# Experts ordered on chip by rising token count, with 64 more rows in the last eight places

## The chip, the cores and the metric

One core of one Trainium2 chip. The metric is device time in microseconds (us) of one execution of the whole kernel, lower is better. Engines by their names in the profile: PE is TensorE (PEld its weight loads), DVE is VectorE, ACT is ScalarE, POOL is GpSimd, SP is SyncE; a name with a small q is that engine's queue.

## What is computed

One layer of an encoder trunk, float32, 1024 tokens of width 1024. A mixer (neighbourhood attention, a bidirectional RWKV-7 scan, cross attention into memory tokens) comes first and is not touched by the change. Behind it stands a mixture of experts:

```python
g_idx = argmax(h2 @ w_group + b_group)                 # 1 of 4 groups
top_p, top_i = top_k(softmax(logits of that group), 2) # 2 of its 4 experts
weights = g_w[:, None] * top_p / sum(top_p)
expert = g_idx[:, None] * 4 + top_i                    # 2 of 16 experts per token
hid = silu(xb @ w_gate[e]) * (xb @ w_up[e])            # 1024 -> 512
y[token] += (hid @ w_down[e]) * weight                 # 512 -> 1024
```

2048 (token, expert) pairs fall on 16 experts, 128 each on average; how many each one gets is known only on chip. An expert's three matrices are 2 MB each.

## The kernel before

The mixer takes the first 690 us or so. Then `out_projection_router` computes the output projection, the rows for the experts and the routing, in four pairs of 128-token tiles. For each pair `place` (line 1690 on) gives every (token, expert) pair a slot, 1024 slots per expert, and GpSimd scatters one entry of eight words per pair into `tok_dram` (line 1576): token row, half-row numbers, weight. `s.count` is kept on VectorE and holds, in the end, each expert's number of rows.

`experts` (line 1824 on) has two parts.

**The fixed part** runs over 16 experts in the order `EXPERTS`: expert i of group 0, of group 1, 2, 3, then i + 1. Each multiplies exactly its first 128 slots; slots that nobody filled hold entries whose writes are dropped. On TensorE expert e is: gate (L2038), transposes of the hidden block of expert e - 1 (`turn_h`, L2016), up (L2046), transposes of the next expert's rows (`turn_x`, L2008), down of expert e - 1 (L2026). Gate and up matrices have three buffers (`GU_SETS`), down matrices two. SyncE loads gate and up of expert e once gate and up of expert e - 3 are done; ScalarE loads down of e once down of e - 2 is done, and does SiLU and the copy of the transposed hidden block. VectorE does the product `hid`, the copy of the transposed rows, and `finish`: weight times product plus the output rows read back. GpSimd's queue holds, per expert: `read_rows` (output rows, L1918), `expert_rows` (gather of input rows, L1821, waits for `turn_x` two experts on), in experts 6 to 13 four `entries` each (a register read and two small DMAs with the slots of a possible overflow block, L1932 to L1934), and `write_rows` (L1924).

**The overflow part** takes what exceeds 128, in blocks of 64 rows. `overflow_blocks` and `overflow_rows` compute on VectorE, early in the fixed part, how many blocks there are and which expert and slots each has (`s.blk`). Every engine then runs a loop of 6 turns with 6 places, each place in an `If` (`overflow`, line 1882 on). A block loads its expert's three matrices again. Its products are 64 rows tall: two halves of the columns go to the two 64-row halves of the result (L2073, L2080, L2097; a block is 32, 32 and 16 matmul instructions in the profile). Blocks are chained by the output: the half rows are read from the output (L1987), summed (L2236), written (L1995), and the next block's read waits for that write.

```python
for q in range(COLS):
    mm = pe.matmul(pg[q * ROW:(q + 1) * ROW, 0:256], xoT[:, j, :], wg[g][:, j, q * 256:(q + 1) * 256],
                   start=(j == 0), stop=(j == KD - 1))
```

Of the kernel before, what the change touches and what calls it, by code (L numbers as in the profile page):

```python
# [62 lines left out]
EXPERTS = [NE // NG * g + i for i in range(NE // NG) for g in range(NG)]  # L63
# [1433 lines left out]
def out_projection_router(nc, s):  # L1497
# [4 lines left out]
    with ExitStack() as c:  # L1502
# [20 lines left out]
        slotf = sb("slotf", [P, 2, 2])  # L1523
        unused = sb("unused", [P, 16, ENTRY], I32)
# [18 lines left out]
        def _(sp):  # L1543
# [8 lines left out]
            for load in expert_loads(s, EXPERTS[0], 0, 0):  # L1552
                load(sp)
            expert_loads(s, EXPERTS[1], 1, 1)[2](sp)
            for t in range(TT):
                if t == TT - 1:
                    sp.wait_ge(done, 2 * TT)
                    for load in expert_loads(s, EXPERTS[1], 1, 1)[0:2]:
# [74 lines left out]
        def _(dve):  # L1633
# [69 lines left out]

            link(dve.memset(unused[:, :, :], 0))
# [62 lines left out]
            place(PAIRS - 1)  # L1767

# [56 lines left out]
def experts(nc, s):  # L1825
# [4 lines left out]
    with ExitStack() as c:  # L1830
# [6 lines left out]
        acc, acc_o = s.proj[:, 2:4, :], s.proj[:, C_ALL - 1, 0:512]  # L1837
        weight = s.idx[:, :, WEIGHT].bitcast(F32)
        idx_u = sb("idx_u", [P, TURN, ENTRY], I32)
# [24 lines left out]
        idx_in = sem("idx_in")  # L1864
        xo_in = [sem(f"xo_in{u}") for u in range(2)]
# [26 lines left out]
        def _(sp):  # L1892
            tok = s.tok_dram.rearrange("(g i r) c -> i r g c", g=NG, i=NE // NG)
# [4 lines left out]
            for e in range(2, NE):  # L1898
                for load, used in zip(expert_loads(s, EXPERTS[e], e % GU_SETS, e % 2)[0:2], (gated, upped)):
                    if e >= GU_SETS:  # L1900
                        sp.wait_ge(used, e - GU_SETS + 1)
                    load(sp)

            def load_weights(b, i, third, turn):
                e = sp.value_load(s.blk[0:1, ds(b, 1)], min_val=0, max_val=NE - 1)
                for load, used in zip(expert_loads(s, e, (NE + turn) % GU_SETS, turn % 2)[0:2], (gated, upped)):
                    sp.wait_ge(used, b + (NE - GU_SETS + 1))
# [4 lines left out]
        def _(pool):  # L1912
# [31 lines left out]

            pool.wait_ge(s.idx_first, 16)
# [5 lines left out]
            pool.wait_ge(s.idx_rest, 16 * NE // NG)  # L1951
# [4 lines left out]
            for e in range(NE):  # L1956
# [10 lines left out]
                if e == NE - 2:  # L1967
                    pool.wait_ge(zeroed, 2)
                    pool.wait_ge(idx_in, 32 * NOV)
                    for b in range(2):  # L1970
                        take(b, b, b + 1)
                        gather(b)
                    pool.sem_inc(xo_turned, 1)
                if e in RECLAIM:
                    pool.drain()
                if e == NE - 1:
                    pool.wait_ge(xo_turned, 2)
                    take(2, 2, 3)
                    gather(2)
                    n = overflow_count(pool)  # L1980
                write_rows(e)
            for g in range(NG):
                pool.wait_ge(s.row_written[g], 16 * NE // NG)

            def rest(b, i, third, turn):
                u = turn % 2
                pool.indirect_dma_start(out=acc_o, out_offset=None, in_=halves,  # L1987
                                        in_offset=bass.IndirectOffsetOnAxis(ap=idx_u[:, turn, HALF_READ:HALF_READ + 1], axis=0)).then_inc(s.half_in[u], 16)
                pool.wait_ge(xo_turned, b + 3)
# [3 lines left out]
                pool.wait_ge(summed_o, b + 3)  # L1993
# [3 lines left out]
                pool.wait_ge(s.row_written_o[u], i * 16 + 16)  # L1997
# [4 lines left out]
        def _(pe):  # L2002
            def turn_x(e):
                pe.wait_ge(x_in[e % 2], e // 2 * 16 + 16)
                if e:
                    pe.wait_ge(x_copied, e)
                for j in range(KD):
                    mm = pe.transpose(pt[:, j // 4, (j % 4) * P:(j % 4 + 1) * P], x[:, e % 2, j * P:(j + 1) * P], s.ident)  # L2008
                mm.then_inc(x_turned, 1)

            def turn_h(e):
                pe.wait_ge(hidden, e + 1)
                if e:
                    pe.wait_ge(h_copied, e)
                for j in range(KF):
                    mm = pe.transpose(ph[:, j * P:(j + 1) * P], hid[:, j * P:(j + 1) * P], s.ident)  # L2016
                mm.then_inc(h_turned, 1)

            def down(e):
                pe.wait_ge(h_copied, e + 1)  # L2020
                pe.wait_ge(wd_in[e % 2], e // 2 * 16 + 16)
                if e:
                    pe.wait_ge(summed, e)
                for half in range(2):
# [4 lines left out]

            turn_x(0)  # L2030
            for e in range(NE):
                u, g = e % 2, e % GU_SETS
                pe.wait_ge(x_copied, e + 1)
                pe.wait_ge(wg_in[g], e // GU_SETS * 16 + 16)
                if e:
                    pe.wait_ge(silu, e)
                for j in range(KD):
                    mm = pe.matmul(pg[:, :], xT[:, u, j, :], wg[g][:, j, :], start=(j == 0), stop=(j == KD - 1))  # L2038
                mm.then_inc(gated, 1)
                if e:  # L2040
                    turn_h(e - 1)
                pe.wait_ge(wu_in[g], e // GU_SETS * 16 + 16)
                if e:
                    pe.wait_ge(hidden, e)
                for j in range(KD):
# [4 lines left out]
                if e:  # L2050
                    down(e - 1)

            def turn_rows(u, part):
                for j in range(4 * part, 4 * part + 4):
                    mm = pe.transpose(pt[:, j // 4, (j % 4) * P:(j % 4 + 1) * P], xo[:, u, j * P:(j + 1) * P], s.ident)
                return mm

            turn_h(NE - 1)
            pe.wait_ge(xo_in[0], 16)
            turn_rows(0, 0)  # L2060
            turn_rows(0, 1).then_inc(xo_turned, 1)
            n = overflow_count(pe)
            down(NE - 1)

            def block_of_rows(b, i, third, turn):
                u, g = turn % 2, (NE + turn) % GU_SETS
                fixed = len(range(g, NE, GU_SETS))
                pe.wait_ge(xo_copied, b + 2)
                pe.wait_ge(wg_in[g], third * 16 + 16 * (fixed + 1))
                pe.wait_ge(silu_o, b + 1)  # L2070
                for j in range(KD):
                    for q in range(COLS):
                        mm = pe.matmul(pg[q * ROW:(q + 1) * ROW, 0:256], xoT[:, j, :], wg[g][:, j, q * 256:(q + 1) * 256],  # L2073
# [326 lines left out]
```

## Time and profile before

| what | value |
|---|---|
| runs shown (3) | 1269.63, 1271.72, 3097.08 us |
| median of the runs | 1271.72 us |
| span of the profiled execution, first to last instruction | 1268.2 us |
| TensorE busy | 1175.8 us, 93% |
| VectorE, ScalarE, GpSimd busy | 551.6, 308.4, 203.2 us |
| moved by the DMA engines | 242.40 MB |
| fixed part of the experts, first gate to last down product | about 821 to 1177 us |
| overflow blocks | 5 |

The profile gives no other time for the profiled execution than its span; launch and end around it are in the runs' times only. Busy times of TensorE are modelled at their ends, so consecutive groups overlap by some 0.2 us; start-to-start times are the better ones. A DMA's duration is from its issue to its landing.

### The profile page before, as it was taken

What the parts mean: (1) busy time and instruction counts of PE and PEld (TensorE: products, weight loads), DVE (VectorE), ACT (ScalarE), POOL (GpSimd) and SP (SyncE); (2) the same over time, 40 slices, a digit from 0 to 9 for tenths busy, and PEclk for the clock granted to TensorE, in tenths of its full rate; (3) what the DMA queues carried; (4) which work ended last, traced back from release to release, by engine and by line L of the source; (5) the groups of instructions that cost most, each with busy time, mean ns of one, the idle gap of its engine ahead of it and who ended that gap; (6) DMA issues with size and microseconds to landing.
All of it is one profiled execution on the core that took longest, in us unless ns stands there. A gap on an engine that the chain in (4) does not pass through costs nothing. (4 is left out here: it accounts for less than half of the span.)

```text
span 1268.2 us, 24058 instructions
## 1 busy us (share of the span) xinstructions
PE 1175.8 (93%) x9814; PEld 660.0 (52%) x9814; DVE 551.6 (43%) x1316; ACT 308.4 (24%) x791; POOL 203.2 (16%) x250
## 2 busy tenths in 40 slices
PE   6999999999998888999999999399999999999785
PEld 5534444444444666899974555244444444444442
DVE  4358356899793555555745344302211111111111
ACT  5153116322212666433431222000000000000000
POOL 0201310300001334000000011401102242332122
PEclk9999999999998999999999999599999999999988
DMA  9311521222203723144344612688989999999973
GB/s 319 99 38 48 180 68 55 103 97 100 51 34 90 187 78 110 50 114 113 104 168 170 265 67 77 238 322 326 368 353 353 365 340 372 347 369 326 390 263 128
DMA packets 110055, 242.40 MB, mean 191 GB/s; under 512 B 36404, under 2 KB 71684, under 8 KB 104568
## 3 DMA queue, kind: packets, MB, share of 16 engines
q1 hardware_dynamic: 82696, 150.30, 33.3%
q0 software_dynamic: 16688, 48.59, 10.9%
q10 hardware_dynamic: 10560, 41.94, 9.9%
q8 instruction: 79, 1.29, 0.4%
q14 instruction: 32, 0.26, 0.1%
HBM read 211.25 MB, written 36.10 MB: 195 GB/s over the span
## 5 line engine op out<-in xcount | busy, mean ns | idle before, releaser
L505 PE MATMUL pj_ps<-hT,pj_w 128*128 128x512 f32 x576 | 253.0, 595 | 0.0
L505 PEld LDWEIGHTS pj_ps<-hT,pj_w 128*128 128x128 f32 x576 | 107.8, 190 | 135.4 <-issue 134.9
L1387 PE MATMUL ps_out<-w_out,mixT 128*128 128x512 f32 x256 | 112.3, 594 | 2.1 <-PEq L2315 1.8
L2026 PE MATMUL ex_py<-wd,ex_hT 128*128 128x512 f32 x256 | 112.6, 593 | 0.2 <-DVE proj L2169 0.2
L2206 DVE TENSOR_TENSOR ex_hid<-ex_pu,ex_sg 128x512 f32<-128x512 f32 x16 | 11.1, 692 | 205.5 <-PE ex_pu L2046 205.5
L2122 ACT ACTIVATE ex_sg<-ex_pg 128x512 f32<-128x512 f32 x16 | 9.6, 597 | 324.4 <-PE ex_pg L2038 324.4
L2038 PE MATMUL ex_pg<-proj 128*128 128x512 f32 x176 | 80.2, 610 | 1.3 <-DVE proj L2162 1.3
L1387 PEld LDWEIGHTS ps_out<-w_out,mixT 128*128 128x128 f32 x256 | 47.8, 190 | 59.5 <-issue 59.4
L715 DVE RECIPROCAL mixT<-mixT 128x1024 f32<-128x1024 f32 (+1 forms) x11 | 68.9, 6262 | 22.5 <-ACT mixT L635 17.5
L2046 PE MATMUL ex_pu<-proj 128*128 128x512 f32 x176 | 77.3, 592 | 0.0
L2026 PEld LDWEIGHTS ex_py<-wd,ex_hT 128*128 128x128 f32 x256 | 47.5, 190 | 54.4 <-issue 54.0
L1576 POOL DMA_INDIRECT slot_tokens<-op_entry,op_slot x16 | 15.6, 975 | 287.9 <-DVE op_slot L1701 284.2
L2169 DVE SCALAR_TENSOR_TENSOR proj<-ex_py,idx,proj 128x1024 f32<-128x1024 f32 x16 | 20.5, 1284 | 91.7 <-PE ex_py L2026 91.7
L2038 PEld LDWEIGHTS ex_pg<-proj 128*128 128x128 f32 x176 | 34.4, 196 | 45.1 <-issue 43.4
L509 PE MATMUL pj_ps<-proj,hT 128*128 128x512 f32 x128 | 55.5, 594 | 0.0
L1924 POOL DMA_INDIRECT out<-proj,idx x16 | 16.4, 1026 | 241.8 <-DVE proj L2169 241.8
L2046 PEld LDWEIGHTS ex_pu<-proj 128*128 128x128 f32 x176 | 32.7, 190 | 37.3 <-issue 37.3
L1277 DVE TENSOR_TENSOR wd<-sc_ps,cst 128x384 f32<-128x384 f32 x64 | 35.7, 557 | 32.1 <-PE sc_ps L1214 31.1
L1210 PE MATMUL sc_ps<-proj 64*64 64x128 f32 x512 | 40.8, 270 | 1.0 <-PEq L1181 1.0
L509 PEld LDWEIGHTS pj_ps<-proj,hT 128*128 128x128 f32 x128 | 24.2, 190 | 30.5 <-issue 30.5
L1077 DVE CUSTOM_DVE_ANT_0 at_ssb<-at_ps_s,at_table 128x253 f32<-128x253 f32 (+1 forms) x64 | 24.0, 408 | 33.3 <-issue 33.3
L1117 ACT ACTIVATE at_pr<-at_ssb,at_nm 128x253 f32<-128x253 f32 (+1 forms) x64 | 31.4, 492 | 21.7 <-DVE at_nm L1077 14.6
(324 smaller groups left out, 1959.2 us busy)
## 6 DMA issues: line engine op xcount, KB each, us to landing
wd<-in_moe_w_down ACTq DMA_DIRECT2D x20, 2048.0 KB
proj<-in_moe_w_gate SPq DMA_DIRECT2D x14, 2048.0 KB, 10.5
proj<-in_moe_w_up SPq DMA_DIRECT2D x14, 2048.0 KB, 9.3
mixT<-in_moe_w_gate SPq DMA_DIRECT2D x7, 2048.0 KB, 10.8
mixT<-in_moe_w_up SPq DMA_DIRECT2D x7, 2048.0 KB
pj_w<-in_w_in SPq DMA_DIRECT2D x18, 512.0 KB, 3.8
proj<-in_x SPq DMA_DIRECT2D x16, 512.0 KB, 10.2
products<-pj_unit POOLq DMA_DIRECT2D x4, 2048.0 KB, 10.1
```

What stands on the lines that cost most here:

```text
L505: mm = pe.matmul(ps[:, t % 2, half, :], w_tile(t)[:, n, :], s.hT[:, n, half * 512:(half + 1) * 512], start=(n == 0), stop=(n == KD - 1))
L509: mm = pe.matmul(ps[:, t % 2, half, :], s.hT[:, n, b * P:(b + 1) * P], w_v[:, n, :], start=(n == 0), stop=(n == KD - 1))
L715: then(dve.reciprocal(std[:, 0:ln], std[:, 0:ln]))
L1077: dve.tensor_tensor_reduce(ssb[R][:, k % 2, 0:n], ps_s[:, k % 2, R, 0:n], table, -1.0, 3.0e38, ALU.add, ALU.min, nm[:, k % 2, R:R + 1]).th ...
L1117: act.activation(pr(x, R)[:, x % 3, 0:n], ssb[R][:, x % 2, 0:n], ACT.Exp, bias=nm[:, x % 2, R:R + 1], scale=-1.0, accum_out=rs[:, x % 3, R ...
L1210: pe.matmul(ps[p0:p1, n, 0, m * P:(m + 1) * P].rearrange("p (f t) -> p f t", f=2), f[p0:p1, n, 2 + m, :], f[p0:p1, n, 0:2, :], start=True, ...
L1277: dve.tensor_tensor(lm[:, i % 2, n, :, :].rearrange("p f c -> p (f c)"), ps[:, n, 0, 0:6 * HD], s.l_mask[UNITS[n][0]], ALU.mult).then_inc( ...
L1387: mm = pe.matmul(s.ps_out[:, t % 2, half * 512:(half + 1) * 512], s.mixT[:, k, t * P:(t + 1) * P], s.w_out[:, k, half * 512:(half + 1) * 5 ...
L2026: mm = pe.matmul(py[:, half, :], hT[:, j, :], wd[e % 2][:, j, half * 512:(half + 1) * 512], start=(j == 0), stop=(j == KF - 1))
L2038: mm = pe.matmul(pg[:, :], xT[:, u, j, :], wg[g][:, j, :], start=(j == 0), stop=(j == KD - 1))
L2046: mm = pe.matmul(pu[:, :], xT[:, u, j, :], wu[g][:, j, :], start=(j == 0), stop=(j == KD - 1))
L2169: dve.scalar_tensor_tensor(out=y[:, e % 2, :], in0=py[:, :, :].rearrange("p a n -> p (a n)"), scalar=weight[:, e:e + 1], in1=acc[:, e % 2, ...
```

## The change

The order of the experts is no longer fixed in the program. Experts 0 and 4 keep the first two places. At the router's end VectorE sorts each group's four experts by `s.count`, the largest last; the places go through the groups in turn, so that the last eight places (`FIRST_ROOM` = 8 on) hold the two largest of every group. `s.order` has the expert of each place and its first slots. SyncE and ScalarE read the expert number from it before each weight load; SyncE loads each place's 128 entries by a DMA of its own (14 of them, before: 4 in the block and one for the first two places, as now), and then the eight places' next 64 entries (two DMAs each).

Each of the last eight places has a room of 64 rows behind its 128 and multiplies it with the same weights, whether slots are filled or not. In the program's order on TensorE a place with a room is: gate, `turn_h_room` of the place before, up, `turn_room`, `down_room` of the place before, gate rows, `turn_h`, up rows, `turn_x` of the next, down. The last place turns one more block of rows (`turn_room(ROOMS)`) for a possible loop block. `overflow_blocks` subtracts 64 from the counts of the experts that have a room (`s.held`). The loop itself stays.

```diff
+STATIC = [NE // NG * g for g in range(2)]
+ROOMS = 2 * NG
+FIRST_ROOM = NE - ROOMS
...
+            def order_experts():
+                per = NE // NG
+                link(dve.scalar_tensor_tensor(out=key[:, :], in0=s.count[:, :], scalar=float(NE), in1=iota16, op0=ALU.mult, op1=ALU.add))
+                link(dve.memset(key[:, 0:len(STATIC) * per:per], -1.0))
...
+                link(dve.tensor_scalar(s.held[:, :], key[:, :], float(per - ROOMS // NG), float(ROW), ALU.is_ge, ALU.mult))
...
+                dve.tensor_copy(s.order[:, :, :], orderf[:, :, :]).then_inc(s.ordered, 1)
...
@@ SyncE
-            sp.dma_start(s.idx[:, 2:NG, :], tok[0, 0:P, 2:NG, :]).then_inc(s.idx_rest, 16)
-            for i in range(1, NE // NG):
-                sp.dma_start(s.idx[:, i * NG:(i + 1) * NG, :], tok[i, 0:P, :, :]).then_inc(s.idx_rest, 16)
+            def load_entries(p):
+                row = sp.value_load(s.order[0:1, 1, p:p + 1], min_val=0, max_val=(NE - 1) * SLOTS)
+                sp.dma_start(s.idx[:, p, :], s.tok_dram[ds(row, P), :]).then_inc(s.idx_rest, 16)
+            def load_room(q):
+                row = sp.value_load(s.order[0:1, 2, FIRST_ROOM + q:FIRST_ROOM + q + 1], min_val=0, max_val=(NE - 1) * SLOTS + P)
+                sp.dma_start(idx_r[0:ROW, q, :], s.tok_dram[ds(row, ROW), :]).then_inc(room_in, 16)
+                sp.dma_start(idx_r[ROW:P, q, 0:NEXT_HALF], s.tok_dram[ds(row, ROW), NEXT_HALF:2 * NEXT_HALF]).then_inc(room_in, 16)
+            sp.wait_ge(s.ordered, 1)
+            for p in range(len(STATIC), NE):
+                load_entries(p)
             sp.wait_ge(s.out_in, 16 * TT)
+            for p in range(len(STATIC), NE):
+                e = sp.value_load(s.order[0:1, 0, p:p + 1], min_val=0, max_val=NE - 1)
...
+                if p == len(STATIC):
+                    for q in range(ROOMS):
+                        load_room(q)
@@ GpSimd, in the loop over places e
-                if e == NE - 2:
+                if e == FIRST_ROOM - 1:
                     pool.wait_ge(zeroed, 2)
+                    pool.wait_ge(room_in, 32 * ROOMS)
+                    for q in range(2):
+                        room_rows(q)
+                if e >= FIRST_ROOM:
+                    read_room(e - FIRST_ROOM)
+                if FIRST_ROOM < e < NE - 1:
+                    room_rows(e - FIRST_ROOM + 1)
                 if e in RECLAIM:
                     pool.drain()
                 if e == NE - 1:
+                    pool.wait_ge(idx_in, 32 * NOV)
+                    for b in range(3):
+                        take(b, b, b + 1)
+                        pool.wait_ge(xo_turned, ROOMS + b - 1)
+                        gather(b)
                     n = overflow_count(pool)
                 write_rows(e)
+                if e >= FIRST_ROOM:
+                    write_room(e - FIRST_ROOM)
@@ TensorE, in the loop over places e
-                if e + 1 < NE:
+                if e >= FIRST_ROOM:
+                    turn_room(e - FIRST_ROOM)
+                else:
                     turn_x(e + 1)
-                if e:
+                if behind_room:
+                    down_room(e - 1 - FIRST_ROOM)
+                elif e:
                     down(e - 1)
+                if e >= FIRST_ROOM:
+                    q = e - FIRST_ROOM
+                    pe.wait_ge(xo_copied, q + 1)
+                    pe.wait_ge(silu, e + 1)
+                    gate_or_up_rows(pg, wg[g]).then_inc(gated, 1)
+                    turn_h(e)
+                    pe.wait_ge(hidden, e + 1)
+                    gate_or_up_rows(pu, wu[g]).then_inc(upped, 1)
+                    if e + 1 < NE:
+                        turn_x(e + 1)
+                    else:
+                        turn_room(ROOMS)
+                    down(e)
+            turn_h_room(ROOMS - 1)
             n = overflow_count(pe)
-            down(NE - 1)
+            down_room(ROOMS - 1)
@@ VectorE, the room's sum
+            def finish_room(q):
+                u = q % 2
+                dve.wait_ge(downed, room_done(q))
+                dve.wait_ge(s.half_in[u], q // 2 * 16 + 16)
+                if q:
+                    dve.wait_ge(s.row_written_o[1 - u], (q - 1) // 2 * 16 + 16)
+                dve.scalar_tensor_tensor(out=yo[:, :], in0=py[:, u, :], scalar=weight_r[:, q:q + 1], in1=acc_o[:, u, :], op0=ALU.mult, op1=ALU.add).then_inc(summed_o, 1)
@@ VectorE, overflow_blocks
-                link(dve.tensor_tensor(over[:, :, :], b3(s.count[:, :].unsqueeze(2), [P, NE, OVERS]), b3(s.limits.unsqueeze(1), [P, NE, OVERS]), ALU.is_gt))
+                link(dve.tensor_tensor(ovn[:, :], s.count[:, :], s.held[:, :], ALU.subtract))
+                link(dve.tensor_tensor(over[:, :, :], b3(ovn[:, :].unsqueeze(2), [P, NE, OVERS]), b3(s.limits.unsqueeze(1), [P, NE, OVERS]), ALU.is_gt))
```

`room_rows(q)` gathers a room's 64 input rows, `read_room(q)` reads its half rows from the output, `write_room(q)` writes them, each one indirect DMA on GpSimd; `gate_or_up_rows` and `down_rows` are the block's products as before, and the semaphore counts that the loop waits for are raised by the rooms'.

## Rows read from the trace of the kernel before

**Rows 1.** The page: span, and each engine's busy time, share, instructions.

```profile
span 1268.2 us, 24058 instructions
...
PE 1175.8 (93%) x9814; PEld 660.0 (52%) x9814; DVE 551.6 (43%) x1316; ACT 308.4 (24%) x791; POOL 203.2 (16%) x250
```

**Rows 2.** Busy us, granted clock, DMA share and GB/s of the steady fixed part.

```profile
870.00:1150.00 280.00, 280.00 (x767) 132.13 (x766) 47.99 (x62) 13.47 (x25) 70.47 (x100) 1.00 0.94 356
```

**Rows 3.** The chain of waits, one expert and the end: start us, us, what.

```profile
1125.44 6.87 PE ex_pg L2038 x16
...
1132.74 6.87 PE ex_pu L2046 x16
1139.61 0.87 PE ex_pt L2008 x8
1140.48 6.87 PE ex_py L2026 x16
1147.35 6.87 PE ex_pg L2038 x16
1154.22 0.44 PE ex_ph L2016 x4
...
1177.00 1.29 DVE proj L2169
```

**Rows 4.** The chain of waits behind the fixed part.

```profile
1179.12 12.57 DMA out<-proj,idx
...
1192.73 9.70 DMA proj<-out,ex_idx_u
...
1260.38 2.36 DMA out<-ex_yo,ex_idx_u
```

**Rows 5.** DMA issues: what, queue, count, KB each, median us to landing.

```profile
proj<-in_moe_w_gate SPq DMA_DIRECT2D x14, 2048.0 KB, 10.5
...
mixT<-in_moe_w_gate SPq DMA_DIRECT2D x7, 2048.0 KB, 10.8
...
out<-ex_yo,ex_idx_u POOLq DMA_INDIRECT x5, 4.1
```

**Rows 6.** TensorE in one overflow block: start us, us, line, count.

```profile
1228.58 3.62 PE L2073 MATMUL ex_pg<-mixT,ex_xoT 128*64 128x256 f32 x32
1232.04 3.62 PE L2080 MATMUL ex_pu<-mixT,ex_xoT 128*64 128x256 f32 x32
1235.59 0.66 PE L2055 MATMUL ex_pt<-cst,ex_xo 128*128 128x128 f32 x4
...
1236.46 0.60 PE L2055 MATMUL ex_pt<-cst,ex_xo 128*128 128x128 f32 x4
1237.10 3.65 PE L2097 MATMUL ex_py<-wd,ex_hoT 128*64 128x512 f32 x16
1240.58 3.62 PE L2073 MATMUL ex_pg<-proj,ex_xoT 128*64 128x256 f32 x32
```

**Rows 7.** GpSimd's entries of one expert, first and last; landing of L1942.

```profile
977.78 0.61 POOL L1933 DMA_DIRECT2D ex_idx_o<-slot_tokens  x1
...
983.58 0.52 POOL L1934 DMA_DIRECT2D ex_idx_o<-slot_tokens  x1
...
DMA to landing us min/median/max: 3.7/8.6/16.3
```

**Rows 8.** Start of the experts: timelines of VectorE, GpSimd, SyncE, TensorE.

```profile
805.17 0.17 DVE L1702 TENSOR_TENSOR count<-op_pl,count 128x16 f32<-128x16 f32 x1
...
809.36 0.97 POOL L1576 DMA_INDIRECT slot_tokens<-op_entry,op_slot  x1 [0.30 <-issue]
...
814.77 0.50 SPq L1814 DMA_DIRECT2D proj<-in_moe_w_gate  x1
...
854.55 1.04 PE L2008 MATMUL ex_pt<-cst,expert_x 128*128 128x128 f32 x8
...
862.29 7.03 PE L2038 MATMUL ex_pg<-proj 128*128 128x512 f32 x16
```

More of the change, by code:

```diff
@@ L62, with fixed_done, room_done @@
 NEXT_HALF = 3
-EXPERTS = [NE // NG * g + i for i in range(NE // NG) for g in range(NG)]
+STATIC = [NE // NG * g for g in range(2)]
+ROOMS = 2 * NG
+FIRST_ROOM = NE - ROOMS
+def fixed_done(p):
+    return p + 1 + max(0, p - FIRST_ROOM)
+def room_done(q):
+    return fixed_done(FIRST_ROOM + q) + 1
+ALL_DONE = NE + ROOMS
 RMS_EPS = 1e-6
@@ L1557, in _ @@
                     sp.wait_ge(done, 2 * TT)
-                    for load in expert_loads(s, EXPERTS[1], 1, 1)[0:2]:
+                    for load in expert_loads(s, STATIC[1], 1, 1)[0:2]:
                         load(sp)
@@ L1767, in _ @@
             place(PAIRS - 1)
+            order_experts()
         @block.scalar
@@ L1864, in experts @@
         idx_in = sem("idx_in")
+        room_in = sem("room_in")
+        held_of = sb("held_of", [P, NOV])
         xo_in = [sem(f"xo_in{u}") for u in range(2)]
@@ L2009, in turn_x, with turn_rows, turn_room @@
                 mm.then_inc(x_turned, 1)
+            def turn_rows(u, part):
+                for j in range(4 * part, 4 * part + 4):
+                    mm = pe.transpose(pt[:, j // 4, (j % 4) * P:(j % 4 + 1) * P], xo[:, u, j * P:(j + 1) * P], s.ident)
+                return mm
+            def turn_room(q):
+                pe.wait_ge(xo_in[q % 2], q // 2 * 16 + 16)
+                pe.wait_ge(x_copied, min(FIRST_ROOM + q + 1, NE))
+                if q == ROOMS:
+                    pe.wait_ge(xo_copied, ROOMS)
+                turn_rows(q % 2, 0)
+                turn_rows(q % 2, 1).then_inc(xo_turned, 1)
             def turn_h(e):
@@ L2017, in turn_h, with turn_h_room @@
                 mm.then_inc(h_turned, 1)
+            def turn_h_room(q):
+                pe.wait_ge(hidden_o, q + 1)
+                pe.wait_ge(h_copied, FIRST_ROOM + q + 1)
+                for a in range(2):
+                    mm = pe.transpose(ph[:, a * P:(a + 1) * P], hido[:, a * P:(a + 1) * P], s.ident)
+                mm.then_inc(ho_turned, 1)
             def down(e):
@@ L2028, in down, with gate_or_up_rows, down_rows, down_room @@
                 mm.then_inc(downed, 1)
+            def gate_or_up_rows(out, w):
+                for j in range(KD):
+                    for q in range(COLS):
+                        mm = pe.matmul(out[q * ROW:(q + 1) * ROW, 0:256], xoT[:, j, :], w[:, j, q * 256:(q + 1) * 256],
+                                       start=(j == 0), stop=(j == KD - 1))
+                return mm
+            def down_rows(u, w):
+                for j in range(KF):
+                    rows = hoT[:, j % 2 * P + j // 2 * ROW:j % 2 * P + (j // 2 + 1) * ROW]
+                    for q in range(COLS):
+                        mm = pe.matmul(py[q * ROW:(q + 1) * ROW, u, :], rows, w[:, j, q * 512:(q + 1) * 512],
+                                       start=(j == 0), stop=(j == KF - 1))
+                return mm
+            def down_room(q):
+                pe.wait_ge(ho_copied, q + 1)
+                pe.wait_ge(summed, FIRST_ROOM + q + 1)
+                down_rows(q % 2, wd[(FIRST_ROOM + q) % 2]).then_inc(downed, 1)
             turn_x(0)
@@ L2300, in hybrid_layer @@
         s.count = top.enter_context(nc.sbuf_tensor("count", [P, NE], F32))
+        s.held = top.enter_context(nc.sbuf_tensor("held", [P, NE], F32))
+        s.order = top.enter_context(nc.sbuf_tensor("order", [P, 3, NE], I32))
         def weights(ap):
```

227 lines of the change are left out of this document (138 added, 89 removed).

## The prediction

> **What bounds the kernel now.** Read the page's busy shares first [rows 1]: TensorE is busy 1175.8 of 1268.2 us, nothing else comes near. A share is an average, so the next view is the table by stretches, for the 280 us in which the experts' fixed part is steady [rows 2]: TensorE 280.00 of 280.00 us at a granted clock of 1.00 (2.4 GHz), the DMA engines 0.94. Two resources are nearly full, so it has to be settled which one sets the pace. The chain of waits does that [rows 3]: one expert is gate 6.87, transposes of the hidden block 0.44, up 6.87, transposes of the next rows 0.87, down 6.87, together 21.92 us, and the next gate starts 21.91 after the last. Not one transfer stands in it. TensorE sets the pace; the DMA engines keep up.
>
> The stage then ends in something else. The last down product is over at 1176.9 (VectorE takes it at 1177.00 [rows 3]); from there to 1268.2 are 91.3 us. The chain there is a string of transfers [rows 4]: the write of the last expert's rows 12.57, and then, per block of the overflow loop, a read of the half rows, a sum, a write. The first of five starts at 1192.73, the last lands at 1262.74, so the five take 70.0, 14.0 each. They are five by the issues: 14 + 7 gate loads are 16 experts and 5 blocks, and `ex_yo` is written five times [rows 5]. After the last landing 5.5 us go to the turns of the loop that do nothing and to the kernel's end.
>
> So the change trades a serial tail against work on the engine that sets the pace. Both have rows.
>
> **What it removes.** The reference's router, worked out on its own inputs, gives expert 1 139 rows, 7 142, 11 133, 12 169, 14 153, all others at most 128. Each of the five exceeds 128 by less than 64: this is the same five as in the trace. Each is among the two largest of its group, and none is expert 0 or 4, which keep the first places, so all five reach the last eight places and the loop gets zero blocks. The 70.0 us of blocks go. Of the rest of the tail, the last write, something takes its place (below); the 5.5 us at the end stay, with one more empty turn. Five turns and the end cost 5.5, so I add 1.0 and take 6.5.
>
> **What it adds on TensorE.** Each of eight places multiplies 64 more rows, filled or not. That work is exactly a block's. In the one that ran without a stall [rows 6] gate takes 3.46 (1228.58 to 1232.04), up 3.55, four transposes of rows with the two of the hidden block 0.87 (1235.59 to 1236.46), four more 0.64, down 3.48; the next gate starts 12.00 after this one. The arithmetic alone would be three times half of 6.87, 10.3, with 0.87 and 0.22 of transposes: 11.4, the lower bound. The 0.6 above it are small pauses where 64-wide and 128-wide products meet (3.55 and not 3.46; 1.51 for ten transposes, where 0.87 for eight in [rows 3] makes 1.09). The new order interleaves the room's parts with those of the 128 rows: down of the room before, gate rows, transposes, up rows, transposes. That gives four or five such meetings per room, about what the block has, so I take 12.00. An upper bound of 13.0 allows 0.2 more at each. Eight rooms are 96.0 us (91 to 104). Nothing hides them: TensorE has no idle time in this stage.
>
> The Trainium skill, TensorEngine Tiling (Array Packing), Key Properties, says that a change of tiling mode drains TensorE; it gives no price, and it speaks against this order. The rows agree that there is a pause, of 0.1 to 0.2 us; should a drain be dearer between long products, rival 2 has the sum.
>
> **What it adds elsewhere in the stage.** VectorE and ScalarE get per room a row copy, a product, a sum, two activations, all under 1.3 us against 33.9 us per expert (21.92 + 12.00); VectorE's next copy of rows is due only behind a down product of 6.87. Hidden. If a room's sum is late, it holds the next down, but it has gate rows, transposes, up rows and transposes of 8.2 us ahead of it. The weight loads now come every 33.9 us in the last eight, so the transfers relax there. Each gate load is still issued three experts ahead.
>
> GpSimd is the queue to watch. Per place it waits for the next rows' transposes, issues the gather of an expert's rows (about 0.4 + 1.0), then in places 6 to 13 the four `entries` (977.78 to 984.10, 6.3) [rows 7], then the read of the room's half rows (1.3) and the gather of the next room's rows. So room 0's gather starts 8.0 us behind these transposes. TensorE reaches the room's transposes after down, gate, 0.44 and up, 21.05: 13.1 us of room. A gather of this kind took 3.7 to 16.3 us to land, 8.6 in the median [rows 7], the longest while weights stream. For the first room, in the full stage, I take 14: 1 us of stall. For the others the margin is 11.5 us; at 8.6 nothing is lost, at 16.3 it would be 4.8 six times, 29 us. I take the median, since the transfers are less dense there: 0. The write of the rows, the last in this queue, is needed two experts later.
>
> In the last place GpSimd first issues the last-but-one room's write, one read and one entry copy before the gather that TensorE needs for the ninth transposes. Counted from the last gate's start: room 6's product ends at 18.4, its sum at 19.4, and the gather starts at about 23.1; with weights no longer streaming I take 4 us to land, 27.2, where TensorE arrives at 26.1. 1.1 us of stall (0 to 6).
>
> **At the start of the stage.** `order_experts` is twelve small VectorE instructions of some 0.2 us, 2.5 us behind 805.34; the block ends only when GpSimd has issued the last scatter (810.33) and it has landed, so they are hidden with some 4 us to spare [rows 8]. SyncE now reads a register and issues a small DMA 14 times, before expert 2's weights, and 8 times two DMAs before expert 3's. GpSimd's four entries give the price: 1.74 for a register with two DMAs, 1.2 with one. So expert 2's weights are issued near 830 instead of 814.77, and are needed at 862.29 [rows 8]. Two matrices of 2 MB at 356 GB/s are 12 us: about 845 with the gathers beside them. The third gather comes 10 us late and lands near 843, needed at 854.55. Expert 3's weights go from 831 and 838 to 844, needed at 884. All hidden: 0, and at twice the price of a register read some 5 us. It may win half a microsecond at the first gather, which no longer meets the weights. Five more small VectorE instructions in the overflow tables are hidden too.
>
> **The sum**, against the profiled execution. Last down product 1176.9 + rooms 96.0 + first gather 1.0 + last gather 1.1 = 1275.0. The last room's down now waits for a copy on ScalarE that nothing covers, 0.6. Then the sum on VectorE, 0.8 with its release; GpSimd's issue, 0.8 behind it as in [rows 4] (1178.29 to 1179.12); the landing of the half rows, 4.1 (the median of five [rows 5]; 2.4 at best, 12.6 for a write of whole rows under load); the end 6.5. Together 1287.8, 19.6 us more than 1268.2. The page lists no other time of the profiled execution; the two lower runs, 1269.63 and 1271.72, lie 1.4 and 3.5 above its span. On the median of the runs shown, 1271.72, this makes 1291.3: 1.5% slower. A measurement of this kernel can tell about 2%, 25 us, so most of this case counts as no change.
>
> **Rivals.**
>
> 1. Room gathers come late. GpSimd's queue becomes the bound at each room's transposes. For it: a 6.3 us block of entries stands ahead, and landings of 14 to 16 us are in the trace. Against it: the gap between weight loads is wider there. At 14 us each, (14 − 11.5) × 6 = 15 us more, 1306; at worst 1320. TensorE would show idle time at the transposes of `ex_xo`. The Trainium skill, Trainium Kernel Development and Optimization, Key Constraints, says that transfers of the SP, ACT and POOL queues run on the same 16 engines and interleave; the landings of 3.7 us alone and 16.3 us under weights agree.
> 2. Changes between 64-wide and 128-wide products cost more when none falls into a wait. At 0.5 instead of 0.2 us, five times in each of eight rooms: 12 us more, 1303.
> 3. Not slower: rooms cost TensorE less than a block did. From [rows 3, 6] the change breaks even where 8 rooms cost no more than 96 − 19.6 = 76.4, 9.5 us each; the place would be the room's own products running beside their neighbours' in the array's free half. At 9.0 a room it gives 1267. Against it: 10.3 of products is exactly half of the full ones, with no pause in it, and the three groups of [rows 6] took 3.46 to 3.55.
> 4. It does not do what it says: a block is left, because the chip's order is another than I take it to be. One block left costs about 14 on top, 1305; all five 70, 1361. The five loads in the trace and the counts agree, so there is little for it.
> 5. SyncE's register reads are dearer than GpSimd's and TensorE waits for expert 2 or 3: at three times the price 10 us, 1301.
>
> **How the numbers follow.** The forecast has 0.64, its own range 1285 to 1297; rival 1 0.17, rival 2 0.08, rival 3 0.04, rival 4 0.05, rival 5 0.02. Slower by over 2% (over 1297.2) is most of rivals 1, 2, 4 and 5: 0.28. Faster by over 2% (under 1246.3) needs a room under 6.5 us, which is less than its products' columns take: 0.02. The rest, 0.70, lies within 2%. The range runs from 1281 (rooms 11.4, writes at 2.4, no stalls) to 1307 (rival 1 at 14 us).
>
> **What would show it.** Right: no `ex_yo` write behind a loop block; 21 gate loads become 16; an expert's period 21.9 in the first eight places and 33.9 in the last eight; last product near 1275; a tail of some 13 us behind it. Wrong: idle time at `ex_xo` transposes (rival 1); periods of over 35 us with TensorE counted busy (rival 2), under 32 (rival 3); gate loads above 16 (rival 4); a gap before the gate at 862 (rival 5).

## The result and the profile after

| | before | after |
|---|---|---|
| median of the runs | 1270.68 us (4 runs) | 1297.01 us (4 runs) |
| profiled execution, span | 1268.2 us | 1297.6 us |
| ratio of the times, 95% interval | | 1.020 (1.017 to 1.023) |
| TensorE busy | 1175.8 us | 1215.9 us |
| moved by the DMA engines | 242.40 MB | 210.90 MB |
| overflow blocks | 5 | 0 |

The change makes the kernel 26.3 us slower at the medians; the forecast was 19.6 us, 1291.3. The profiled execution after took 1299.35 us, 1.8 above its span. One run before took 3097.08 us and is no measure of the kernel; the ratio leaves it out, and without it the median before is 1269.63 and the difference 27.4 us.

The page of the kernel after: the engine line stands against [rows 1]; the two lines of DMA issues against [rows 5].

```profile
span 1297.6 us, 24797 instructions
...
PE 1215.9 (94%) x10084; PEld 681.0 (52%) x10084; DVE 562.2 (43%) x1341; ACT 310.3 (24%) x797; POOL 208.0 (16%) x239
...
proj<-in_moe_w_gate SPq DMA_DIRECT2D x11, 2048.0 KB, 10.3
...
mixT<-in_moe_w_gate SPq DMA_DIRECT2D x5, 2048.0 KB, 10.3
```

11 + 5 gate loads are 16, and no `out<-ex_yo,ex_idx_u` write is left: the loop gets nothing to do. 31.5 MB fewer are moved, and the kernel is slower all the same.

Stretches of the kernel after (columns as in [rows 2]: stretch, length, busy PE, PEld, DVE, ACT, POOL, granted clock, DMA share, GB/s). The first is the steady part without rooms, the second is six places with rooms from gate to gate, the others lie around the two waits for gathers.

```profile
870.00:990.00 120.00, 120.00 (x331) 56.52 (x330) 24.82 (x43) 6.51 (x12) 20.85 (x25) 1.00 0.95 372
1040.00:1243.67 203.67, 203.67 (x901) 101.72 (x900) 30.41 (x36) 11.11 (x24) 57.68 (x77) 1.00 0.58 212
...
1010.00:1015.00 5.00, 2.02 (x7) 0.71 (x6) 0.69 (x1) 0.00 (x0) 0.83 (x1) 0.99 0.42 113
1015.00:1020.00 5.00, 5.00 (x14) 3.01 (x14) 0.69 (x1) 0.00 (x0) 0.00 (x0) 0.66 0.00 0
...
1266.00:1275.00 9.00, 4.52 (x38) 2.89 (x37) 0.42 (x1) 0.73 (x2) 2.69 (x6) 0.96 0.83 224
```

TensorE is full in both long stretches, at full clock. With rooms the DMA share falls from 0.95 to 0.58: the rooms push the transfers off the limit without giving TensorE anything for it.

TensorE's timeline of the kernel after (start, us, what; in brackets the idle time before and what ended it): the first room, with the parts of one place with a room from gate 1039.98 to gate 1073.93, and the last place. [rows 3, 6] are what they answer to.

```profile
1004.80 7.03 PE L2182 MATMUL ex_pu<-proj 128*128 128x512 f32 x16
1014.81 1.88 PE L2098 MATMUL ex_pt<-cst,ex_xo 128*128 128x128 f32 x8 [2.98 <-DMA ex_xo<-ffn_rows,ex_idx_r]
1016.49 7.96 PE L2135 MATMUL ex_py<-wd,ex_hT 128*128 128x512 f32 x16
1024.38 3.67 PE L2142 MATMUL ex_pg<-proj,ex_xoT 128*64 128x256 f32 x32
...
1039.98 7.03 PE L2170 MATMUL ex_pg<-proj 128*128 128x512 f32 x16
...
1053.93 1.04 PE L2098 MATMUL ex_pt<-cst,ex_xo 128*128 128x128 f32 x8
1054.90 3.65 PE L2150 MATMUL ex_py<-wd,ex_hoT 128*64 128x512 f32 x16
1058.39 3.62 PE L2142 MATMUL ex_pg<-proj,ex_xoT 128*64 128x256 f32 x32
1061.94 0.66 PE L2116 MATMUL ex_ph<-cst,ex_hid 128*128 128x128 f32 x4
1062.53 3.67 PE L2142 MATMUL ex_pu<-proj,ex_xoT 128*64 128x256 f32 x32
...
1073.93 1.45 PE L2170 MATMUL ex_pg<-mixT,proj 128*128 128x512 f32 x3
...
1266.22 3.67 PE L2142 MATMUL ex_pu<-proj,ex_xoT 128*64 128x256 f32 x32
1274.37 1.97 PE L2098 MATMUL ex_pt<-cst,ex_xo 128*128 128x128 f32 x8 [4.48 <-DMA ex_xo<-ffn_rows,ex_idx_u]
1276.14 7.85 PE L2135 MATMUL ex_py<-wd,ex_hT 128*128 128x512 f32 x16
1283.82 0.38 PE L2123 MATMUL ex_ph<-cst,ex_hido 128*128 128x128 f32 x2
1285.46 3.65 PE L2150 MATMUL ex_py<-wd,ex_hoT 128*64 128x512 f32 x16 [1.25 <-DVE proj L2316]
```

Three things are to be seen. A place takes 33.95 from gate to gate, 21.92 + 12.03: the room costs what the block did. Transposes of 64 gathered rows wait twice, and never in between (1053.93: no bracket): 2.98 us for the first room's rows, and 4.48 us for the ninth set, which is not a room's but that of a possible loop block. And what follows each wait is slow as well: transposes 1.68 and 1.77 where they take 0.97 at 1053.93, down 7.89 and 7.68 (to the next start) where it takes 6.87. The table by stretches shows why: the granted clock is 0.99 in the stretch with the wait and 0.66 in the 5 us behind it, so for part of them TensorE ran at 1.2 GHz.

Why the first room's rows came late is in GpSimd's timeline of the kernel after (the write of rows, the last of the entries, the gather), and the same write stands so in the kernel before (last line, from its own timeline):

```profile
999.85 1.03 POOL L1979 DMA_INDIRECT out<-proj,idx  x1 [12.05 <-DVE proj L2316]
...
1007.84 0.52 POOL L1989 DMA_DIRECT2D ex_idx_o<-slot_tokens  x1
1008.67 0.94 POOL L2004 DMA_INDIRECT ex_xo<-ffn_rows,ex_idx_r  x1 [0.30 <-issue]
...
996.14 1.04 POOL L1924 DMA_INDIRECT out<-proj,idx  x1 [12.03 <-DVE proj L2169]
```

GpSimd issues in the order of its program. The write waits 12.05 us for VectorE's sum behind a down product, and everything behind it in the queue waits too: the gather leaves 3.16 us before TensorE wants its rows (1011.83).

The end in the chain of waits of the kernel after (start us, us, what), against [rows 4]:

```profile
1266.71 7.62 DMA ex_xo<-ffn_rows,ex_idx_u
...
1289.15 0.76 DVE ex_yo L2360
...
1290.73 1.00 POOL out L2017
```

One write is issued at 1290.73 where five blocks used to be, and 6.87 us later all is over. Its transfers are done by 1293.0 (the DMA share is 0.40 from 1292.5 to 1293.0 and 0.00 behind that), so 4.6 us follow the last transfer.

### The profile page after: what moved, and what is told of

Read it like the earlier page. It is cut to its first block and busy times, and to the rows that moved or that the text cites. A ratio compares the mean times of both kernels' runs of the same rounds, so it can differ in the third digit from the quotient of the medians.

```text
span 1297.6 us, 24797 instructions
## 1 busy us (share of the span) xinstructions
PE 1215.9 (94%) x10084; PEld 681.0 (52%) x10084; DVE 562.2 (43%) x1341; ACT 310.3 (24%) x797; POOL 208.0 (16%) x239
## 2 busy tenths in 40 slices
DMA packets 108139, 210.90 MB, mean 163 GB/s; under 512 B 38352, under 2 KB 73632, under 8 KB 103928
## 6 DMA issues: line engine op xcount, KB each, us to landing
proj<-in_moe_w_up SPq DMA_DIRECT2D x11, 2048.0 KB, 13.3
```

## The experiments

"From the first gate" below is the span less the start of the first expert's gate. It takes out the mixer and the router, where the change does nothing and where the executions differ by themselves (below). Where no number of runs is given there is one. All times "beside" are medians of the kernel before on the same chip.

**Three baselines.** Both kernels once more, unedited.

`before_again`, 

> The kernel before, unedited, for the time at which its experts start. In the nine traces of changed kernels the first gate starts between 821.84 and 826.51, in the one trace of the kernel before at 821.26. Theory (the stages ahead of the experts, which no edit touches, vary by some 5 us from run to run with the granted clock): this run's first gate may lie anywhere from 820 to 827. Rival (the change itself delays the experts by 3 us): 820 to 822.

`before_third`, 

> The kernel before once more, for the same question: first gate anywhere from 820 to 827 by the theory of the clock, 820 to 822 by the rival.

`after_again`, 

> The changed kernel, unedited. The first gate anywhere from 820 to 827 by the theory, 824 to 826 by the rival; from the first gate to the last product 464 us by both, since the two waits for gathers belong to the kernel and not to the run.

Measured: before 1268.48 and 1275.16 us, after 1295.51. The first gate starts at 823.79 and 830.70 before, 821.77 after (821.26 and 825.03 in the first pair): it moves by 9.4 us between runs of the kernel before alone, and the kernel after lies inside that. The 830.70 is later than the theory allowed (820 to 827), and further still from the rival (820 to 822). From the first gate: before 446.9 (the execution that the prediction used), 443.0, 442.8; after 472.6 and 471.9. Behind the first gate the change costs 26 to 30 us by these executions, and the executions after repeat to 0.7 us, waits included:

```profile
1011.15 1.97 PE L2098 MATMUL ex_pt<-cst,ex_xo 128*128 128x128 f32 x8 [2.88 <-DMA ex_xo<-ffn_rows,ex_idx_r]
...
1270.57 1.97 PE L2098 MATMUL ex_pt<-cst,ex_xo 128*128 128x128 f32 x8 [4.40 <-DMA ex_xo<-ffn_rows,ex_idx_u]
```

The five blocks took 70.0 us in the execution that the prediction used, 66.7 and 67.6 in the other two: what the change removes was 2.4 to 3.3 us smaller than it looked.

**The first room's gather: place in the queue, or transfers?**

```diff
@@ GpSimd, in the loop over places e
-                if 6 <= e < 14:
-                    for b in range((e - 6) * NOV // 8, (e - 5) * NOV // 8):
-                        entries(b)
...
                 if FIRST_ROOM < e < NE - 1:
                     room_rows(e - FIRST_ROOM + 1)
+                if 6 <= e < 14:
+                    for b in range((e - 6) * NOV // 8, (e - 5) * NOV // 8):
+                        entries(b)
```

> In GpSimd's queue the room's read and gather go ahead of the four entries of a place. Theory A (the queue sets when the first room's rows come): the gather is issued about 5 us earlier, TensorE's 2.98 us of idle time at the first room's transposes is gone, and with it the half clock behind it; eighth place's gate to ninth place's gate falls from 42.5 to about 38 us; whole kernel 4 to 5 us shorter. Rival B (the transfers set it: weights stream and a gather lands when the weights have landed): the gather is issued earlier but lands later by as much, idle time stays over 2 us.

Measured: 1293.06 us beside 1268.9, 469.5 from the first gate. GpSimd's and TensorE's timelines of this kernel:

```profile
999.71 0.91 POOL L2004 DMA_INDIRECT ex_xo<-ffn_rows,ex_idx_r  x1 [0.30 <-issue]
...
1009.54 1.09 PE L2098 MATMUL ex_pt<-cst,ex_xo 128*128 128x128 f32 x8 [1.86 <-DMA ex_xo<-ffn_rows,ex_idx_r]
```

The gather is issued right behind the gather of the expert's rows, ahead of the entries that stand between the two in the kernel after; counted to where TensorE wants the rows, it leaves 4.8 us earlier (8.0 us ahead of that, in place of 3.2). It lands after 9.8 us instead of 6.1. The wait shrinks by 1.1 us of the 2.98 only, so the outcome lies between theory and rival, nearer the rival: most of the head start is lost in the transfer. While this gather was on its way the weights were streaming (DMA share 1.01 in the first 5.3 us behind its issue, against 0.53 over the 6.1 us of the gather in the kernel after). The write is still ahead of it in the queue (issued 995.70 after 12.33 us of waiting), and this run does not move that. But behind 1.86 us of idle TensorE is at full speed (transposes 1.09, down 6.96), so this place is 2.8 us shorter in all.

**The last gather: out of TensorE's way.** In the last place down of the 128 rows goes ahead of the transposes for a possible block.

```diff
@@ TensorE, last place (VectorE alike: finish(e) before copy_rows())
-                        turn_room(ROOMS)
-                    down(e)
+                        down(e)
+                        turn_room(ROOMS)
@@ GpSimd, e == NE - 1: take(2, 2, 3) and gather(2) behind write_rows and write_room
```

> In the last place the ninth transposes stand behind the down product of the 128 rows and no longer ahead of it, and GpSimd's third gather for the loop behind the last writes. Theory A (the 4.48 us of idle time is a wait for rows that only a loop block would need): the idle time falls to 0 and the two slowed groups behind it (transposes 1.8, down 7.7) run at full clock; last product about 6 us earlier, counted from the first gate. Rival B (the wait only moves, to the last room's down product, which needs the same engine's sums): under 2 us.

Measured: 1288.46 us beside 1268.9, 464.7 from the first gate, last product after 456.0 where the kernel after needs 463.9. TensorE's only wait in the last place is now

```profile
1274.54 3.65 PE L2154 MATMUL ex_py<-wd,ex_hoT 128*64 128x512 f32 x16 [0.47 <-ACT ex_hoT L2251]
```

The last product comes 7.9 us sooner: 6.1 are the wait with its slow products, 0.8 the shorter wait ahead of the last down, and the rest lies at the first gate and the first room, which the edit does not touch. These 6.9 us bought nothing here: the rows turned there are for a loop block, and there is none.

**Why was that gather late?** ScalarE issues the down load of a possible first block 0.3 us behind it (1267.03), 2 MB that nobody will use. Here it is issued later.

```diff
@@ ScalarE, behind the last place
-            load_down(0, 0, room_done(ROOMS - 2))
             finish_room(ROOMS - 1)
+            load_down(0, 0, room_done(ROOMS - 2))
```

> ScalarE's load of a down matrix for a loop block that does not exist goes behind the last copy. Theory C (this 2 MB load, issued 0.3 us behind the gather, is what makes the gather take 7.6 us to land): the gather lands in about 4 us, TensorE's idle time in the last place falls from 4.5 to about 1. Rival (the landing is long for other reasons, the write and read ahead of it in GpSimd's queue): it stays at 7 us and more.

Measured: 1297.15 us beside 1268.9, 469.9 from the first gate, last product after 458.0. GpSimd, TensorE and ScalarE in this kernel's timeline:

```profile
1266.60 0.94 POOL L1997 DMA_INDIRECT ex_xo<-ffn_rows,ex_idx_u  x1 [0.27 <-issue]
...
1270.63 1.09 PE L2098 MATMUL ex_pt<-cst,ex_xo 128*128 128x128 f32 x8 [0.84 <-DMA ex_xo<-ffn_rows,ex_idx_u]
...
1291.13 0.30 ACT L2289 ACTIVATE ex_sg<-ex_sg 128x1 f32<-128x1 f32 x2 [11.86 <-DMA wd<-in_moe_w_down]
```

Without that load the same gather lands in 4.0 us instead of 7.6, and the wait is 0.84 instead of 4.48 (4.40 in `after_again`): the load was the cause. Other small gathers are on their way in both cases. The last product comes 5.9 us sooner (part of it from a shorter first wait, 2.42, in this execution), and only 2.7 us of that reach the end, since the kernel now ends on the load itself (issued at 1279.61, in at 1291.1). A transfer that nobody needs costs time on either side: beside one that is needed, or as the last to land.

**Both waits gone.** `turn_last`, and the first two room gathers three places earlier.

```diff
@@ GpSimd, on top of turn_last
-                if e == FIRST_ROOM - 1:
+                if e == FIRST_ROOM - 4:
                     pool.wait_ge(zeroed, 2)
```

> Eight rooms. The gathers of the first two rooms are issued four places ahead and not one, and the last place has its transposes behind the down product as in the run before. Theory (the 9 us between forecast and measurement in the stage are two waits for gathers with the half clock behind them, nothing else): no wait at a gather left on TensorE; first gate to last product 464 us falls to 452 to 454; the kernel lands at 1284 to 1289, still 12 to 18 above the kernel before, because eight rooms cost 96 and save 70. Rival (something else in the order on chip costs as much): over 1292.

Measured: 1286.73 us (4 runs) beside 1272.66 (9 runs), ratio 1.013 (1.010 to 1.017). TensorE never waits for a gather; last product after 452.0, against 355.6 + 96.2 = 451.8. Even with every wait for a gather gone the change loses 14 us at the medians: the price is the rooms themselves.

**How many rooms?** Only 5 of the 8 hold rows. The number was changed alone, to 12, and to 4 (the largest of each group: experts 1, 7, 11, 12; expert 14 keeps a block; the same line with a 4).

```diff
-ROOMS = 2 * NG
+ROOMS = 12
```

> Twelve rooms, four more than in the change, none of the four ever filled. Theory (each room is 12.0 us of TensorE with no cover, filled or not): 48 us more than with eight, about 1345; twelve periods near 33.9. Rival (part of the cost is fixed, or hides behind weights once the transfers are slack): 30 us more or less, under 1330.

Measured: 1353.66 us; last product after 516.4, 52.5 more than with 8. Four rooms at 12.03 are 48.1. The time is 9 us over the 1345 expected, 4.4 of it between the first gate and the last product: both waits and the products behind them are longer, less a shorter first gate. The first wait is the larger part, with down behind it at 9.0 instead of 6.87 (timeline of TensorE in this kernel):

```profile
929.83 1.97 PE L2098 MATMUL ex_pt<-cst,ex_xo 128*128 128x128 f32 x8 [5.68 <-DMA ex_xo<-ffn_rows,ex_idx_r]
931.60 9.10 PE L2135 MATMUL ex_py<-wd,ex_hT 128*128 128x512 f32 x16
940.62 3.67 PE L2142 MATMUL ex_pg<-mixT,ex_xoT 128*64 128x256 f32 x32
```

No entries stand ahead of the first room's gather here, and it is late all the same: it is issued at 916.03, behind a write that waited 18.33 us for VectorE's sum, and takes 13.8 us to land.

> Rooms in the last four places only; the largest expert of each group has one, the expert with 153 rows does not, so one block is left to the loop. Theory A (each room is 12.0 us of TensorE with no cover, each block about 14 us of tail, the first one more for the write ahead of it): 48 us less of rooms, about 20 to 25 more of tail; 1297 - 25 = about 1270, equal to the kernel before or slightly under it (1258 to 1272). Rival (rooms are not additive, most of the loss is a fixed cost of the order on chip): it stays above 1285.

Measured: 1260.1 us (4 runs) beside 1268.9 (7 runs), ratio 0.992 (0.990 to 0.995). The same code with half the rooms is faster than the kernel before, by 0.8%.

**What a room's time consists of.** Gate and up of the rooms over 2 of the 8 slices, down over 2 of the 4; this leaves out most of the rooms' sums, and the output lacks them.

```diff
             def gate_or_up_rows(out, w):
-                for j in range(KD):
+                for j in (0, KD - 1):
...
             def down_rows(u, w):
-                for j in range(KF):
+                for j in (0, KF - 1):
```

> Eight rooms with all their transposes, copies, gathers and writes, but gate and up products over two of eight slices and the down product over two of four; the rooms' sums are left incomplete. Theory (the products themselves set the cost, three times 3.46): gate and up give back three quarters, down one half, 6.9 us per room, 55 us in all; period 27.0; about 1242. Rival (the pauses at changes between 64-wide and 128-wide work set it, or GpSimd's queue takes over as the bound): period stays at 30 or more, 1265 and more.

Measured: 1254.76 us, last product after 418.1. TensorE's timeline of one place (1062.12 to 1090.19), and the gates of a later one:

```profile
1062.12 7.03 PE L2170 MATMUL ex_pg<-mixT,proj 128*128 128x512 f32 x16
...
1077.03 1.09 PE L2098 MATMUL ex_pt<-cst,ex_xo 128*128 128x128 f32 x8 [0.80 <-DMA ex_xo<-ffn_rows,ex_idx_r]
...
1090.19 7.03 PE L2170 MATMUL ex_pg<-proj 128*128 128x512 f32 x16
...
1172.65 7.03 PE L2170 MATMUL ex_pg<-proj 128*128 128x512 f32 x16
...
1199.70 7.03 PE L2170 MATMUL ex_pg<-proj 128*128 128x512 f32 x16
```

The first of these places takes 28.07 instead of 33.95, 0.80 of it a new wait; the later one has no wait and takes 27.05, as expected (27.0). So the products that were left out were worth 6.90 us; worked out from their parts they are 3/4 of 3.5 twice and half of 3.5, 7.0. The room's time is its products' time, to a tenth. The total is 13 us over the 1242 expected, for the most part because TensorE waits longer for gathers once it is less full: 0.80, 0.60 and 0.26 us in three of the places, 2.85 at the first and 10.49 at the last gather, with slow products behind these two.

**The better version.** Four rooms with both edits of `early8`.

> Four rooms with both edits. Theory: the 6 to 8 us of waits and half clock in the run with four rooms go as well; about 1252 to 1255, 1.1 to 1.4% under the kernel before. Rival (with a loop block to come, the ninth transposes and what they release only move behind the down product and the block starts later by as much): 1258 to 1260.

Measured: 1252.77 us (5 runs, 1250.3 to 1256.27) beside 1272.66, ratio 0.985 (0.982 to 0.988): 1.5% faster than before, with an interval well clear of 1, and 44 us under the change as made. The end in TensorE's timeline and then in the chain of waits:

```profile
1225.32 1.04 PE L2102 MATMUL ex_pt<-cst,ex_xo 128*128 128x128 f32 x8
...
1227.05 3.65 PE L2154 MATMUL ex_py<-wd,ex_hoT 128*64 128x512 f32 x16 [0.47 <-ACT ex_hoT L2251]
1230.54 3.62 PE L2146 MATMUL ex_pg<-mixT,ex_xoT 128*64 128x256 f32 x32
...
1239.31 3.65 PE L2154 MATMUL ex_py<-wd,ex_hoT 128*64 128x512 f32 x16 [0.21 <-ACT ex_hoT L2289]
```

```profile
1241.64 3.75 DMA proj<-out,ex_idx_u
...
1247.11 2.38 DMA out<-ex_yo,ex_idx_u
```

The one block follows the last room without a pause, since its weights were loaded beside the rooms: 12.3 us from 1230.54 to the last product at 1242.8, then 11.8 to the end of the span. Fixed part 355.6, four rooms 48.1, block 12.3 and end 11.8 make 427.8 from the first gate; measured 428.1.

## Why the prediction held, and where it was off

The time, 1297.01, lies at the upper edge of the forecast's own range (1285 to 1297) and well inside the whole range (1281 to 1307), 5.7 us above the forecast. (The low end of the whole range adds up to 1282.7 by its own terms, not 1281.) By the steps of the prediction, counted from the first gate to the last product, forecast 454.3, measured 463.9:

| step | forecast | measured |
|---|---|---|
| blocks left | 0 | 0 |
| eight rooms | 8 × 12.00 | 8 × 12.03, clock 1.00 |
| stall at the first gather | 1.0 | 2.98 + 1.7 slow products behind it |
| six room gathers between | 0 | 0 |
| stall at the last gather | 1.1 | 4.48 + 1.6 slow products behind it |
| last room's down waits | 0.6, for ScalarE's copy | 1.25, for VectorE's sum of the 128 rows |
| start of the experts' part | hidden | hidden (third gate 40.97 after the first, before 41.03) |
| last product to the end | 12.2 | 8.7 |

**Held.** That TensorE sets the pace and hides nothing; that work on it costs in full whether its rows are filled or not; that a room costs what an undisturbed block does [rows 6]; that the serial tail goes. `rooms12` and `rooms4` show the first three by their own sizes, `cut` shows that the room's time is its products. On VectorE, ScalarE and SyncE what was called hidden was: SyncE issues 14 loads of entries from 817.68 to 832.4, expert 2's weights at 833.15, and the gate at 866.00 does not wait.

**Mis-sized: the two gather waits.** They were priced as stalls alone, 1.0 and 1.1, and measured 4.7 and 6.1 with what follows. For the first room two errors nearly cancelled, so that the small stall forecast was in part luck. The forecast has the gather start 8.0 us behind the transposes, with 13.1 us left, and land after 14. It started at 1008.67, 18.0 us behind their end (990.63), with 3.2 us left, and landed after 6.1: some 10 us later and 8 us faster, which leaves the 2.0 us between 1.0 and 2.98. What the forecast passed over is the write of rows that stands ahead of the read, the gather of an expert's rows and the entries; it named that write as the last in the queue, needed late, and did not ask what waits behind it. It waits for the sum of the expert before, which comes behind the down product that follows those transposes; the kernel before shows the same wait (12.03 us). Further on the write does not stand in the way: the third room's gather is issued 9.5 us behind its transposes and leaves 11.4 us, as forecast (11.5). The role of the write is read from these timelines; no run moved the write alone. `gather_first` shows that issue and landing can't be added freely: an earlier issue meets the weights and lands later. For the last gather the step "with weights no longer streaming I take 4 us to land" failed. Weights were streaming: ScalarE loads for a loop block before it knows whether there is one. The step looked only at the queue that issues the gather and not at what the other queues send in the same microsecond. The rest of that step was right: the gather was issued 23.0 us behind the last gate (forecast 23.1). Without the load it does land in 4.0 (`load_after`).

**Not priced: what a stall leaves behind.** Behind these two waits the transposes and down took 1.6 to 1.7 us longer than at full speed; behind the 1.86 of `gather_first`, nothing. To the forecast such a wait was its own length and no more.

**Another wait than forecast, at the last room's down.** It ended on VectorE's sum of the 128 rows, since down of these rows comes just ahead. ScalarE's copy, which the forecast had in mind, is what that product waits for where down was moved ahead: 0.47 (`turn_last`).

**Mis-sized the other way: the end.** The forecast added landing (4.1) and end (6.5) as they stood in the kernel before. From issue to the last instruction it was 6.87: at most 2.3 until the transfers were done, 4.6 behind them. Each was taken some 2 us too long, which makes 3.5 us too much in all once the issue (1.8 behind the product, forecast 1.6) is counted.

**Base.** The blocks removed were priced from an execution in which they took 70.0 us, against 66.7 and 67.6 in two others. Between the two profiled executions the account closes: 19.6, + 9.6 for the waits and the rooms' 0.03 each, − 3.5 for the end, + 3.8 for a later first gate, make 29.5; the spans differ by 29.4. The 3.8 is in the stage ahead of the change, and was 2.0 the other way between two other executions (823.79 before, 821.77 after), so it is no cost of the change. Against the two other executions of the kernel before the change costs 3.9 us more behind the first gate than against the one used. What of this scatter stands in the medians, 26.3, the single executions don't tell.

**The rivals.** 1 (room gathers late): partly. It named the right kind of wait, but seven of the eight rooms' gathers were in time, and the second wait was for a gather that no room needs. 2 (dearer changes of product shape): no, 0.03 per room over the forecast. The Trainium skill, TensorEngine Tiling (Array Packing), Key Properties, has a drain at each change of tiling mode; the parts of a place follow each other here at 33.95 in all, so whatever it costs was in the 12.00 already; no run here shows it by itself. 3 (rooms cheaper): no, four more cost 12 each. 4 (a block left): no. 5 (dear register reads): no.

## What to carry to other kernels

Work that is moved to the engine that sets the pace costs its full time, empty rows included, so count how many of the added units will hold something: eight rooms of 12.0 us against five blocks of 13.3 to 14.0 lose, four rooms for the four fullest win. Work for a branch that may not be taken (a prefetch, rows turned ahead) belongs behind the last thing that is needed, in every queue; it cost about 7 us here. When a gather is priced, look at what stands ahead of it in its queue and what each of these waits for, at what the other queues send at that moment, and add to a stall of several microseconds the slow products behind it.

## What the runs showed of the hardware that was not expected

- A gather of 64 rows landed in 7.6 us with one unrelated 2 MB load issued 0.3 us behind it and in 4.0 without that load; the same instruction for the first room took 6.1 us at a DMA share of 0.53, and 9.8 us where the share was 1.01 for the first 5.3 us. Over the eight of the kernel after it was 5.0 at least, 8.3 in the median, 9.4 at most.
- TensorE was slow behind the longer of these waits, and not behind the short ones. Behind 0.84, 0.97 and 1.86 us: eight transposes in 1.09. Behind 2.42 to 10.49: 1.44 to 1.97, and the following down 7.6 to 9.1 instead of 6.87, together 1.5 to 3.0 us on top of the wait. What comes on top did not grow with the wait: 3.0 behind 2.85 us and 2.6 behind 10.49, both in `cut`. The granted clock was 0.66 in the 5 us behind each wait of the kernel after, and 1.00 in the 2.5 us behind the wait of 1.86.
- The same instructions ahead of the change's first edit took up to 9 us more or less from one execution to the next. The granted clock from 60 to 80 us was 0.83 in the profiled execution of the kernel after and in `before_third`, which have the latest first gates of the five unedited executions (825.03 and 830.70), and 1.00 in the other three. That is a part of it: 20 us at 0.83 lose some 3.4 us (an estimate), and the rest stays open. Differences of a few microseconds between two executions had to be read from the first gate on.
